# Twelve of 14 recurrence-input columns as products of rounded parts, and head pairs taken from two key groups

## What is computed

```python
for l in range(DEPTH):
    u = rmsnorm(x, ln1_w[l])
    proj = u @ w_in[l]
    rw = token_shift(proj[..., :RWKV_COLS], rwkv_mu[l])
    zr, zk, zv, zw, za, zg = split_cols(rw, RWKV_SPLITS)
    ...
    o_a = rwkv7_mixer(zr, zk, zv, zw, za, zg, ...)
    o_b = nsa_mixer(nq, nkc, nvc, nks, nvs, nkw, nvw, ngate, ...)
    o_c = swa_sink_mixer(sq, sk, sv, swa_sinks[l], swa_tbl)
    merged = g_a * (o_a @ w_br_a[l]) + g_b * (o_b @ w_br_b[l]) + g_c * (o_c @ w_br_c[l])
    x = x + merged @ w_out[l]
    x = x + peer_ffn(rmsnorm(x, ln2_w[l]), ...)
```

## Time and profile before

| what | value |
|---|---|
| median of three executions | 3841.6 us (3841.47, 3841.6 and 6449.8) |
| the profiled execution, its own time | 3832.32 us |
| its span in the trace | 3830.5 us |
| mean granted TensorE clock of the span | 0.991 of full speed |
| DMA in the span | 912.76 MB, mean 238 GB/s |

### The profile page before, as it was taken

The page is one execution under the profiler, slowest core; times in us unless marked ns, Lnnn a source line. Parts: engine busy times, 40 slices in busy tenths (PEclk is TensorE's granted clock), DMA queues, the critical chain, the costliest instruction groups (busy, mean ns, idle before and its releaser), DMA issues. The chain is left out here.

```text
span 3830.5 us, 65039 instructions
## 1 busy us (share of the span) xinstructions
PE 3600.1 (94%) x25058; PEld 3118.0 (81%) x25058; DVE 2533.2 (66%) x5089; ACT 1597.5 (42%) x3547; POOL 753.0 (20%) x802
## 2 busy tenths in 40 slices
PE   9999999999999999999999999888899999988887
PEld 7888776788788876998779999777787798987776
DVE  5878657677755567655556776776564667676765
ACT  5222546323332346543345444444432554444443
POOL 0000222000000004000000345444300004454442
PEclk9999999999999999999999999999999999999999
DMA  6555311355433431554225899999942269999998
GB/s 275 198 189 185 103 63 67 116 187 183 153 121 135 137 107 45 210 183 166 83 100 209 349 420 421 420 421 421 419 160 113 103 248 368 421 420 421 420 421 352
DMA packets 137765, 912.76 MB, mean 238 GB/s; under 512 B 16487, under 2 KB 16743, under 8 KB 36592
## 3 DMA queue, kind: packets, MB, share of 16 engines
q0 software_dynamic: 97280, 619.14, 40.2%
q1 hardware_dynamic: 40176, 289.47, 20.7%
HBM read 904.05 MB, written 5.28 MB: 237 GB/s over the span
## 5 line engine op out<-in xcount | busy, mean ns | idle before, releaser
L3117 PE MATMUL ps<-arena 128*128 128x128 f32 x6560 | 828.1, 282 | 136.5 <-ACT arena L3186 135.7
L3117 PEld LDWEIGHTS ps<-arena 128*128 128x128 f32 x6560 | 786.1, 195 | 185.4 <-ACT arena L3186 178.6
L3303 POOL DMA_INDIRECT arena<-peer_uv,arena x410 | 455.8, 1112 | 1302.7 <-PE ps L3117 512.9
L3332 DVE CUSTOM_DVE_ANT_0 arena<-arena 128x1024 f32<-128x1024 f32 x410 | 502.7, 1226 | 262.1 <-DMA arena<-peer_uv,arena 255.9
L716 DVE TENSOR_TENSOR w_lo<-wt,w_hi 128x1024 fp32r<-128x1024 f32 x389 | 476.5, 1225 | 297.5 <-ACT w_hi L698 272.8
L698 ACT ACTIVATE w_hi<-wt 128x1024 fp32r<-128x1024 f32 x389 | 408.6, 1061 | 575.1 <-PE ps L751 544.9
L751 PE MATMUL ps<-h_hi,w_hi 128*128 128x512 f32 (+1 forms) x1744 | 635.6, 366 | 6.5 <-ACT h_hi L956 3.5
L751 PE MATMUL ps<-h_hi,w_lo 128*128 128x512 f32 (+1 forms) x1744 | 625.3, 360 | 0.0
L751 PE MATMUL ps<-h_lo,w_hi 128*128 128x512 f32 (+1 forms) x1744 | 586.7, 361 | 0.5 <-DVE h_lo L976 0.5
L751 PEld LDWEIGHTS ps<-h_hi,w_hi 128*128 128x128 f32 x1744 | 329.7, 189 | 67.9 <-issue 12.4
L751 PEld LDWEIGHTS ps<-h_hi,w_lo 128*128 128x128 f32 x1744 | 329.6, 189 | 50.4 <-issue 1.1
(11 more groups left out here) (379 smaller groups left out, 5323.4 us busy)
## 6 DMA issues: line engine op xcount, KB each, us to landing
wt<-wstream SPq DMA_DIRECT2D x245, 1024.0 KB, 4.8
ada_t<-adastream POOLq DMA_DIRECT2D x128, 512.0 KB, 3.6
arena<-wstream SPq DMA_DIRECT2D x18, 1024.0 KB, 7.6
arena<-adafirst SPq DMA_DIRECT2D x8, 1024.0 KB, 18.1
arena<-peer_uv,arena POOLq DMA_INDIRECT x410, 19.2
arena<-bias_by_query POOLq DMA_DIRECT2D x2, 3072.0 KB, 14.7
bias_by_query<-bias_by_distance POOLq DMA_DIRECT2D x1, 4096.0 KB, 17.1
hT<-hT POOLq DMA_DIRECT2D x104, 32.0 KB, 1.7
```

Source lines behind the costliest of these rows:

```text
L3117: ins = pe.matmul(y_banks(t)[m // 4][:, (m % 4) * P:(m % 4 + 1) * P], row[:, D + m * P:D + (m + 1) * P], diag[n % DIAGS], start=s == 0 and ...
L3303: pool.indirect_dma_start(out=rows[at % GB], out_offset=None, in_=peer_uv, in_offset=bass.IndirectOffsetOnAxis(ap=experts[:, t, s:s + 1], ...
L3332: dve.tensor_tensor_reduce(u, u, ztok[:, t], 1.0, 0.0, ALU.mult, ALU.add, hbuf[:, t, s:s + 1]).then_inc(dot_ready.sem, 1)
```

## The change

1. Of the 14 columns of the recurrence's input, all but the first two (12 and 13) are made of rounded parts. ScalarE writes the high part of the normed activations in two halves (n_hi) and of each of the 12 weight columns (128x1024 each); VectorE writes the two halves of n_lo and the low parts of split columns 0, 3, 6 and 9; GpSimd writes the low parts of the other eight. There are three buffers for weight parts, so the high part of split column j waits until TensorE has begun column j - 2. Activations' parts lie in the unused context half of xT and hT.
2. The weights for "wa" and "g2" stand behind column 7 in the stream, in one tile, and the gate's up-projection keeps its place behind column 0.
3. Queries are reordered on the host so that a pair has one head of one key group and one of another. The doubling products and their copies go: four in b's input, four a layer in the NSA input, and two a layer at the end of pe_cmp_swa with the wait before them. Weights, sinks and bias columns are permuted to match.
4. The raw buffer of the mix has two places instead of four.

```diff
-AFTER_MIX = {6: "rwkv_wa", 0: "rwkv_g2"}
+AFTER_MIX = {7: ("rwkv_wa", "rwkv_g2")}
+PLAIN_MIX = 2
+DVE_LOWS = (0, 3, 6, 9)
...
+        def act_in_high(act, l, *js):
+            for j in js:
+                n = in_count(l, j)
+                tile = NTH[PLAN.index(("w_in", l, 0, SPLIT_MIX[j] * P, 1)) // W_TILE]
+                act.wait_ge(w_full[tile % W_SLOTS], 16 * (tile // W_SLOTS + 1))
+                if n >= 3:
+                    act.wait_ge(in_free, in_from + n - 2)
+                act.activation(in_bufs[n % 3][0], in_raw(l, j), ACT.Copy).then_inc(in_raised, 1)
+
+        def low_part(eng, l, j):
+            n = in_count(l, j)
+            hi, lo = in_bufs[n % 3]
+            eng.wait_ge(in_raised, in_from + n + 1)
+            eng.tensor_tensor(lo, in_raw(l, j), hi.bitcast(F32), ALU.subtract).then_inc(in_split[j in DVE_LOWS], 1)
...
         def pe_rwkv_in(pe, W, mm, l):
             def project(n):
+                if n not in SPLIT_MIX:
+                    pe_project(pe, W, mm, "w_in", l, [n * P], LAT, lambda _: D_, hT, parts_ready=n == MIX_ORDER[0])
+                    return
...
+                pe.wait_ge(in_split[j in DVE_LOWS], in_lows(l, j, j in DVE_LOWS))
...
+                for k in range(DC):
+                    W.next("w_in", l, k * P, n * P)
+                    f = slice(k * P, (k + 1) * P)
+                    pe.matmul(bank[:, 0:LAT], hi[:, f], n_hi[:, k], start=k == 0, stop=False)
+                    ins = pe.matmul(bank[:, 0:LAT], hi[:, f], n_lo[:, k], start=False, stop=False)
+                    if k == 0 and c:
+                        ins.then_inc(in_free, 1)
+                    mm(bank[:, 0:LAT], lo[:, f], n_hi[:, k], False, k == DC - 1, D_.full if k == DC - 1 else None)
...
         def act_rwkv_in(act, step, l):
+            for half in range(2):
...
+                act.activation(n_hi[:, ks], hT[:, ks, 0:LAT], ACT.Copy).then_inc(h_hi_ready.sem, 1)
+            act_in_high(act, l, 0, 1, 2)
             act.wait_ge(to_act.sem, to_act.due(act))
...
+            act_in_high(act, l, 3, 4)
...
+            act_in_high(act, l, 5, 6, 7)
...
+            act_in_high(act, l, 8)
...
+            act_in_high(act, l, 9)
...
+            act_in_high(act, l, 10, 11)
...
+        def pool_rwkv_in(pool, l):
+            for j in [j for j in range(len(SPLIT_MIX)) if j not in DVE_LOWS]:
+                low_part(pool, l, j)
...
+            low_part(dve, l, 0)
             mix(12, 13)
             dve.sem_inc(to_act.sem, 1)
-            mix(4, 5, 6, 7)
+            mix(4)
+            low_part(dve, l, 3)
+            mix(5, 6, 7)
+            low_part(dve, l, 6)
...
             mix(1, 2)
+            low_part(dve, l, 9)
...
-            pe_doubled(pe, mm, l, (2,))
...
-            pe_doubled(pe, mm, l, (3,))
...
-            pe.wait_ge(mix_ready.sem, mix_ready.due(pe))
-            for g in range(2):
-                pe.wait_ge(D_.free, D_.given_back())
-                mm(D_.claim()[:, 0:LAT], const("sel", g, P)[ROWS[g], :], fS[ROWS[g], 4, :]).then_inc(D_.full, 1)
...
-                            mm(s[:, x, :], qB[r, u, q * P:(q + 1) * P], kD[r, u // 2, :], inc=SB.scored if x else None)
+                            mm(s[:, x, :], qB[r, u, q * P:(q + 1) * P], kB[r, u // 4, :], inc=SB.scored if x else None)
```

More of the change, by code:

```diff
@@ L70, with by_head @@
 B_COLS = [D, D + P, *range(0, D, P)]
+B_ORDER = [8 * (c // 4) + 4 * x + c % 4 for c in range(8) for x in range(2)]
+N_ORDER = [4 * x + u for u in range(4) for x in range(2)]
+def by_head(order, a, axis, width=HD):
+    a = np.asarray(a)
+    shape = a.shape[:axis] + (len(order), width) + a.shape[axis + 1:]
+    return np.take(a.reshape(shape), order, axis).reshape(a.shape)
 def weight_plan():
@@ L338, in ring @@
             return Ring(sem(name + "_full"), sem(name + "_free"), bufs)
+        with ExitStack() as split:
+            x_rounded, h_rounded = (split.enter_context(nc.sbuf_tensor(name, [P, DC, TOK], F32R))
+                                    for name in ("x_rounded", "h_rounded"))
         xT = sb("xT", [P, DC, TOK])
@@ L368, in model_kernel @@
             merged_lo = part("merged_lo", DC, LAT)
+        with ExitStack() as split:
+            part("under_in", 16 * 3 * P + 16 * 1024)
+            in_w = part("in_w", 3, 2, GROUP * P)
         arena = sb("arena", [P, ARENA])
@@ L625, in dve_norm @@
             for k in range(DC):
-                dve_normed_chunk(dve, hT[:, k, seg], k, seg, v(gain, first + k)).then_inc(h_ready.sem, 1)
+                dve_normed_chunk(dve, hT[:, k, seg], k, seg, v(gain, first + k)).then_inc(xn_ready.sem, 1)
         def modulate(act, l, which, T, k):
@@ L1544, in dve_b_qkv @@
                     dve_turned(dve, step, i - 2, B_OUTS[i - 2][0])
[L1545 to L1552, removed]
                 dve_normed(dve, step, i, *B_OUTS[i])
@@ L1775, in pe_rwkv_in @@
             pe.wait_ge(act_ready.sem, act_ready.due(pe))
[L1776 to L1779, removed]
+            W.wait_for("rwkv_wa", l, 0, 0, width=4)
+            lora(W.standing("rwkv_wa", l, 0, 0, width=4), 12, ROWS)
+            project(7)
+            W.next("rwkv_wa", l, 0, 0, width=4)
+            gates_up = W.next("rwkv_g2", l, 0, 0, width=4)
+            project(0)
+            lora(gates_up, 13, [slice(0, P)])
             for n in (1, 2):
@@ L1836, in mix @@
                 for n in cols:
-                    raw = zraw[:, place[0] % 4]
+                    raw = zraw[:, place[0] % 2]
                     place[0] += 1
@@ L1846, in mix @@
                                                   op0=ALU.mult, op1=ALU.add))
+            for half in range(2):
+                ks = slice(half * DC // 2, (half + 1) * DC // 2)
+                dve.wait_ge(h_hi_ready.sem, h_hi_ready.due(dve))
+                dve.tensor_tensor(n_lo[:, ks], hT[:, ks, 0:LAT], n_hi[:, ks].bitcast(F32), ALU.subtract
+                                  ).then_inc(h_ready.sem, 1)
+            low_part(dve, l, 0)
             mix(12, 13)
             dve.sem_inc(to_act.sem, 1)
-            mix(4, 5, 6, 7)
+            mix(4)
+            low_part(dve, l, 3)
+            mix(5, 6, 7)
+            low_part(dve, l, 6)
             for m in range(RC):
@@ L2392, in pe_nsa_in @@
                 for half in range(2):
-                    mm(bank[half * HD:(half + 1) * HD, 0:30], w[:, 0:HD], hidc[:, 0, k, :], k == 0, k == 1,
-                       D_.full if k and half else None)
-            pe_doubled(pe, mm, l, (3,))
+                    mm(bank[half * HD:(half + 1) * HD, 0:N_CMP], w[:, 0:HD],
+                       hidc[:, 0, k, half * N_CMP:(half + 1) * N_CMP], k == 0, k == 1, D_.full if k and half else None)
             pe.wait_ge(act_ready.sem, act_ready.due(pe))
@@ L2605, in pe_rel @@
                             mm(n_banks[i % 2][:, x, j * LAT:j * LAT + nk], qsrc[r, u, q * P:(q + 1) * P],
-                               key[r, u // 2, 0:nk], inc=SN.scored if x and j == parts - 1 else None)
+                               key[r, 0:nk], inc=SN.scored if x and j == parts - 1 else None)
                 project_gate(GATES_AT[i][0])
@@ L3631, in pack @@
         assert arrays[k].shape[0] == 1
+    qb = arrays["b_w_qkv"]
+    arrays["b_w_qkv"] = np.concatenate([by_head(B_ORDER, qb[:, :, :D], 2), qb[:, :, D:]], 2)
+    arrays["b_w_o"] = by_head(B_ORDER, arrays["b_w_o"], 1)
+    w_in = arrays["w_in"].copy()
+    for at, width in ((IN["nq"], HD), (IN["ngate"], 3), (IN["sq"], HD)):
+        cols = slice(at, at + 8 * width)
+        w_in[:, :, cols] = by_head(N_ORDER, w_in[:, :, cols], 2, width)
+    arrays["w_in"] = w_in
+    for k in ("w_br_b", "w_br_c"):
+        arrays[k] = by_head(N_ORDER, arrays[k], 1)
     for k, n in (("a_w_qkv", 2 * D), ("b_w_qkv", D + 256)):
```

79 lines of the change are left out of this document (42 added, 37 removed).

## The result

The kernel after takes 3850.76 us (median of 14 executions, 3846.83 to 3855.19) where the one before takes 3842.42 beside it (median of 14). The ratio is 1.0021, 95% interval 1.0014 to 1.0029: slower by 8.3 us, or 0.21%, well inside 2%. The forecast was 3848.6, out of a head-pair part of -7.4 and an input stage of +14.4 us in both layers.

What follows compares the result with a forecast made beforehand. TensorE, busy 94% of the span, bounds the kernel, but VectorE meets it at the input stage's end; -7.4 (head pairs) + 14.4 (input stages) = +7.0 us, 3839.3 on the profiled execution, median 3848.6 us; 80% range 3831 to 3862.

Steps and rivals of the forecast that it cites:

- Rival (a): Recurrence's input: VectorE runs on while GpSimd works; -9.2 us in all, 3832.4 us; chance 0.27.
- Rival (b): Recurrence's input: GpSimd's subtraction takes 3.7 us; +19.6 us in all, 3861.2 us; chance 0.12 together with (d).
- (d): Recurrence's input: parts are late and TensorE waits column by column; size inside (b), chance 0.12 together with it.
- The guess from rows: GpSimd's 128x1024 subtraction for a low part: 4 x 0.57 = 2.3 us, between bounds of 1.5 and 3.7 us.
- VectorE's standing behind GpSimd: Input stage: each GpSimd low part steals some 1.8 us from VectorE's full queue; 4.5 x 1.8 = 8.1 us a layer.
- The split without GpSimd's reading: Input stage without any quarrel between engines: VectorE's end moves by -2.0 - 1.4 + 2.5 = -0.9 us a layer.
- 4 x 0.57 = 2.3 us earlier less 0.3 for late first parts: Input stage: column 7, the fourth split one, has its copy 2.0 us earlier.
- part 2: Input stage: work added on the other engines; ScalarE's 14 copies, 15 us a layer, counted as nothing, at most 1 us.
- DMA is busy 0.46 of the stage: Input stage: the weight stream keeps its number of tiles; the moved small weights are wanted 8 us after issue.
- nearly 5 us earlier: End of the input stage, no quarrel between engines: TensorE would be done nearly 5 us earlier and waits for VectorE.
- The head pairs: Dropped doubling products and copies: 2.45 us a layer, 4.9 in both, plus 2.5 in b's input; 7.4 us gained.
- (c): Recurrence after TensorE's wait at the stage's end: lower granted clock, up to +1.8 us a layer, 3852 us; chance 0.06.

Runs made afterwards that it cites:

- e2: Against the kernel after, GpSimd's eight low-part instructions work on 8 columns each and the third product takes the high part; 3836.52 us, ratio to before 0.9979.
- e5: Against the kernel after, GpSimd fills its eight low parts with zeros (writes, reads nothing) in place of the subtraction; 3835.36 us, ratio to before 0.9979.
- e1: Against the kernel after, no column is split; head pairs and the new order of the weights stay; 3835.35 us, ratio to before 0.9978.
- e7: Against the kernel after, all twelve low parts are made by GpSimd and none by VectorE; 3854.72 us, ratio to before 1.0026.

## Why the prediction was right

**The mechanism.** It was the one with 0.55 of the chances: VectorE's two-input operations stand behind GpSimd's, TensorE waits at the meeting. e2 and e5 take the reading away and 16 us go; the trace shows the standing in single operations, as announced. Rival (a), no exclusion, is refuted by the same rows. Rival (b), a slow GpSimd, is refuted by its durations: 2.36 us at least, mean 2.6 with waiting in it, none at 3.7. Of (d), TensorE waiting column by column for parts, the first layer has 4.3 and 0.3 us, in front of a queue on VectorE that was full anyway. The guess from rows was 2.3, the trace's shortest is 2.36. The estimate from the Trainium skill (GPSIMD Engine Reference, section Elementwise) was 2.25, and the trace agrees within 0.1 us.

**The input stage.** Forecast +7.2 a layer. Against e1, which has the same clock in the first layer, it is 68.42 - 60.65 = +7.8 and 68.19 - 60.51 = +7.7. Its two terms:

- VectorE's standing behind GpSimd, forecast 4.5 x 1.8 = 8.1 a layer. From e5 to after it is 9.1 in the first layer and 7.2 in the second, 8.2 on average. Behind column 7 VectorE stood 1.40 + 2.05 + 1.38 + 2.02 = 6.9 us in the first layer (lines 1915 and 1916 at 1792.18, 1794.06, 1810.08 and 1811.92) for low parts 7, 8, 10 and 11: 1.7 each, forecast 1.8. (That 1.8 was loosely got: 5.3 of 36 us off 2.3 would be 2.0, and the 36 us also hold 4.4 us of operations with one SBUF input, lines 1852, 1857, 1864 and 1868, which were left out of the count without a reason.) Low part 5, counted half, cost all of it: the 2.61 us at 1782.84 held the copy of column 7 by 2.2. Together 9.1. Three more long operations, at 1768.27, 1770.35 and 1779.69, belong to low parts 1, 2 and 4 in the idle front, as said; VectorE had nothing due there but columns that it would have waited for.
- The split without GpSimd's reading, forecast -0.9 a layer. e5 against e1: -1.4 in the first layer, +0.5 in the second. The step that failed is "4 x 0.57 = 2.3 us earlier less 0.3 for late first parts". In the first layer of e5 column 7 is copied 22.5 us after the norm's start, where e1 has 25.0: 2.5 earlier, better than said. In the second it is 24.0 against 24.8, only 0.8 earlier. The waits of the second layer's stage, of after, point at the reason:

```profile
ACT in_w L1754 <- DMA wt<-wstream: 10.4, 3, 5.5
...
DVE in_w L1761 <- ACT in_w L1754: 4.4, 1, 4.4
```

The high part of a column needs the weight tile earlier than the plain product did, and the tile is not there: ScalarE waits 10.4 us in three goes (3.8 in one go in the first layer), and VectorE waits 4.4 us for ScalarE. In e5, the kernel compared here, it is 10.7 us in three goes against 5.5 in two, and VectorE's wait is 4.4 as well. No run had the tiles earlier, so that this is the cause is argued and not shown. "Count nothing, at most 1 us a layer" for part 2's ScalarE was right for the first layer and short for the second. "DMA is busy 0.46 of the stage" was an average that did not answer this: the stream has room on the whole, and a tile wanted sooner than it lands is late all the same.

**TensorE's gain.** At the meeting it is idle for 5.0 us, as announced, but the agreement of the numbers is partly luck. The "nearly 5 us earlier" was said of a kernel without quarrel, which is e5: there TensorE is done 54.7 us behind the norm's start, where e1 needs 61.1, so 6.4 us earlier, and waits 4.8. In after it is done at 63.6, later than in e1; on the way it stood 4.3 us for low part 9. The prediction had said that waits between columns would be under 2 us each.

**The head pairs.** Forecast -7.4, measured -8.4 by the medians (interval of the ratio: -5 to -12). By the stretches in the traces the two layers give 2.4 each, forecast 2.45, and b's input 2.9 to 3.5, forecast 2.5. These stretches rest on a single trace of before.

**The clock, (c).** The low grant came, and twice a stage, not only at its end: in the first layer TensorE stood 4.3 us for low part 9 and 5.0 at the meeting, and was granted 0.50 behind both; in the second it stood 3.55 and 4.9. The split column behind low part 9 took 5.1 us (1806.0 to 1811.1), where 24 products at 0.12 are 2.9. But no price shows: behind low part 9 VectorE's queue is full anyway, and behind the meeting the recurrence's start goes at VectorE's pace too. From the bonus' end to the scaling of the keys (line 2165, after's 2246) it is 6.9 us before and 6.8 after in the first layer. To the last copy of the recurrence's results it is 69.1 and 68.8 us before and 69.7 and 69.0 after, and e1, granted 1.00 there in the first layer, has 70.0 and 69.2. The price of +1.8 a layer was wrong; it came from a stage whose front is TensorE's.

**The sum.** 3842.4 - 8.4 + 16.5 = 3850.5, against 3841.6 - 7.4 + 14.4 = 3848.6. Both terms were one or two us too small, and of opposite sign; that they nearly cancel is luck. The 2.2 us between the forecast and the measured median are less than the interval of the ratio (0.0008 x 3842 = 3 us to either side).

## What to carry to other kernels

Before work is moved to an idle engine, find in the timeline where its idle time and the receiver's full queue lie: here VectorE was busy for 63% of the stage, but its queue was full in the half that set the end. Beside a VectorE queue of two-input operations, an elementwise GpSimd operation that reads SBUF is no helper: here a part of 2.4 us took 1.4 to 2.2 us from VectorE, which does the same work in 1.2. Split only as many columns as the idle stretch of the parts' maker holds, and ask for each new reader of a streamed tile when the tile lands, not how busy the stream is.

## What the runs showed that was not expected

- Some operations with one SBUF input stand behind GpSimd too. In e7 line 1945, a 128x1024 operation of one input, took 2.74 us where it takes 0.69 (0.68 ns an element, half of the two-input operations' 1.2), beside a GpSimd operation; four of 128x256 (line 1929) took 3.4 us in place of 1.4. The prediction had counted only two-input operations. The copy from PSUM kept its mean of 0.42 to 0.43 us in both kernels.
- The scan stands as well: 4 instructions took 4.91 us in the second layer of after (at 2837.28) and 2.87 in the first.
- The wait is inside the recorded duration, on both engines, and not in front of it: an operation that waits for this shows as long and busy, and no view of waits names it. That is why VectorE's busy share rose from 63% to 87% of the first layer's stage with 7.4 us of new work.
- The granted clock behind the norm's 2 us wait differed between profiled executions with the same instructions in front (0.57 to 0.67, or 1.00; what decides it stays open), and is worth 1.7 us. A stage of one trace that begins so is not to be compared with another without that row.
